# Moving softmax and gate exponentials from PSUM to SBUF in a two-block transformer kernel

## The reference

```
s = einsum('bqkgd,bskd->bkgqs', qblk, keys) * ATTN_SCALE
p = softmax(s, axis=-1)
o = einsum('bkgqs,bskd->bqkgd', p, vals)
```

```
la    = log_sigmoid(r @ w_d + b_d) / 16
bcum  = cumsum(la)                         # within a chunk
o     = (q * exp(bcum)) @ S  +  att @ v     # att: decayed q k^T, masked
S     = exp(b_last) * S + (k * exp(b_last - bcum))^T @ v
```

## Time and profile before

| | us |
|---|---|
| median of 3 runs | 4646.35 |
| lowest, highest | 4640.53, 4651.82 |
| the profiled execution, its own time | 4640.53 |
| its span, first to last instruction | 4638.7 |
| PE busy | 4180.4 (90%) |
| POOL busy | 1790.5 (39%) |
| DVE busy | 1612.5 (35%) |
| ACT busy | 1024.4 (22%) |
| mean granted clock of TensorE | 0.932 of full speed |

### The profile page before, as it was taken

How to read it: one execution, slowest core, us unless ns; L and a number is a source line. 1 busy time by engine, 2 the same in 40 slices (tenths; PEclk the granted TensorE clock), 3 DMA queues, 4 the chain that set the end, 5 groups by cost and what they waited for, 6 DMA issues and landing times. The chain is left out here.

```text
span 4638.7 us, 54497 instructions
## 1 busy us (share of the span) xinstructions
PE 4180.4 (90%) x20233; PEld 3195.3 (69%) x20233; DVE 1612.5 (35%) x2553; ACT 1024.4 (22%) x1739; POOL 1790.5 (39%) x770
## 2 busy tenths in 40 slices
PE   6899999999899987798999998886988988988999
PEld 5677788888789876566777776664854554866844
DVE  1333334655511141433255553343133334121100
ACT  1333122122200011333122221002144343001100
POOL 1333343233254452343544336664511110876700
PEclk7999999999999988899999998888888887999999
DMA  6111221111155532122322213233311100333332
GB/s 173 40 47 44 76 45 48 41 44 44 62 107 101 103 104 63 38 50 51 79 53 55 51 48 84 71 90 99 94 30 30 30 26 0 94 101 73 95 77 72
DMA packets 511988, 305.18 MB, mean 66 GB/s; under 512 B 37721, under 2 KB 492770, under 8 KB 511162
## 3 DMA queue, kind: packets, MB, share of 16 engines
q1 hardware_dynamic: 499706, 282.43, 24.9%
q10 hardware_dynamic: 12096, 20.33, 1.2%
HBM read 276.42 MB, written 26.27 MB: 65 GB/s over the span
## 5 line engine op out<-in xcount | busy, mean ns | idle before, releaser
L813 POOL TENSOR_TENSOR whi<-ring,con 128x1024 fp32r<-128x1024 f32 (+2 forms) x383 | 892.9, 2331 | 2572.1 <-DMA ring<-in_w_in 2087.0
L507 PE MATMUL ps<-xT_parts,whi 128*128 128x512 f32 (+2 forms) x2600 | 995.4, 383 | 124.0 <-DVEq L1945 71.7
L507 PE MATMUL ps<-hT_parts,whi 128*128 128x512 f32 (+1 forms) x2856 | 1047.8, 367 | 0.0
L507 PE MATMUL ps<-xT_parts,ring_parts 128*128 128x512 f32 (+2 forms) x2600 | 946.2, 364 | 0.0
L815 POOL TENSOR_TENSOR ring_parts<-ring,whi 128x1024 fp32r<-128x1024 f32 (+2 forms) x383 | 899.8, 2349 | 30.0
L1474 ACT ACTIVATE arena<-ps 128x512 f32<-128x512 f32 (+10 forms) x575 | 306.6, 539 | 2407.4 <-PE ps L507 1602.5
L507 PE MATMUL ps<-arena_parts,whi 128*128 128x512 f32 (+1 forms) x2112 | 630.8, 376 | 98.6 <-DVE arena_parts L1983 56.1
L507 PE MATMUL ps<-arena 128*128 128x128 f32 (+10 forms) x3324 | 675.9, 348 | 41.0 <-DVE arena L1951 36.4
L507 PEld LDWEIGHTS ps<-xT_parts,whi 128*128 128x128 f32 (+1 forms) x2600 | 495.9, 191 | 222.1 <-DVEq L1945 63.7
L507 PEld LDWEIGHTS ps<-hT_parts,whi 128*128 128x128 f32 x2856 | 543.5, 190 | 98.0 <-issue 8.4
L507 PEld LDWEIGHTS ps<-arena 128*128 128x128 f32 (+3 forms) x3324 | 450.7, 195 | 190.5 <-issue 138.5
(11 more groups left out here) (136 smaller groups left out, 3654.4 us busy)
## 6 DMA issues: line engine op xcount, KB each, us to landing
ring<-in_w_in SPq DMA_DIRECT2D x504, 256.0 KB, 3.9
arena<-in_w_ada SPq DMA_DIRECT2D x64, 256.0 KB, 4.9
ring<-in_w_up SPq DMA_DIRECT2D x64, 256.0 KB, 3.9
ring<-in_w_down SPq DMA_DIRECT2D x64, 256.0 KB, 3.9
ring<-in_w_out SPq DMA_DIRECT2D x48, 256.0 KB, 3.8
gates_kept<-stage ACTq DMA_DIRECT2D x24, 384.0 KB, 3.9
arena<-gates_kept SPq DMA_DIRECT2D x24, 384.0 KB, 3.6
ring<-in_w_ada SPq DMA_DIRECT2D x32, 256.0 KB, 3.9
```

Source lines behind the costliest of these rows:

```text
L507: return nc.tensor.matmul(o, l, r, start=first, stop=last)
L813: v.tensor_tensor(hi, raw, ones[:, 0:m].unsqueeze(1).to_broadcast([P, kt, m]), ALU.mult).then_inc(w_rounded, 1)
```

## The change

- The exponential of the attention scores is written to `prob` in SBUF; DVE's multiplication then works in place in `prob`. `scores(t)` waits for exp_done in place of prob_done, and the wait for a free `prob` slot goes from DVE to ACT.
- `gE` becomes an SBUF buffer. ACT's exponential reads the sums from PSUM and writes them there; `decayed` reads it there. `exponents` waits for e_ready in place of qk_ready, `levels` for e_ready as well, and ACT's `exponentials(j)` for qk_ready of the unit before.
- `decays` moves from after the second token tile to behind all of them; on ACT `copy_values(gv)` moves ahead of the decay chain.
- PE's wait for wd_in moves from `decays` to the start of the layer's GLA, ahead of `all_read()` and of the queries' tile.

```diff
+        gE = take(9, P)
...
-        gE = bank(2, 9 * P).rearrange("p (c m) -> p c m", c=9)
...
-                        pe.wait_ge(prob_done, u0 + t)
+                        pe.wait_ge(exp_done, u0 + t)
...
                 turned_tile(hP, ALL, m=32)
+                pe.wait_ge(wd_in, 64 * (l + 1))
                 all_read()
...
-                    def decays():
-
-                        pe.wait_ge(wd_in, 64 * (l + 1))
-                        pe.wait_ge(grs_ready, hh * 2)
-                        pe.wait_ge(s_ready, u0)
-                        for d in range(2):
-                            for t in range(NT):
-                                last = mm(bank(4 + 2 * d, 1024)[:, t * P:(t + 1) * P], gr[0:33, t * P:(t + 1) * P],
-                                          gwd[0:33, d, i * P:(i + 1) * P], True, True)
-                        last.then_inc(dec_done, 1)
-
-                    two_token_tiles(NT, {1: [decays]})
+                    two_token_tiles(NT)
+
+
+                    pe.wait_ge(grs_ready, hh * 2)
+                    pe.wait_ge(s_ready, u0)
+                    for d in range(2):
+                        for t in range(NT):
+                            last = mm(bank(4 + 2 * d, 1024)[:, t * P:(t + 1) * P], gr[0:33, t * P:(t + 1) * P],
+                                      gwd[0:33, d, i * P:(i + 1) * P], True, True)
+                    last.then_inc(dec_done, 1)
                     turned_tile(hP)
...
-                        pe.wait_ge(qk_ready, u0 + j)
+                        pe.wait_ge(e_ready, u0 + j)
                         pe.wait_ge(kN_ready, u0 + j)
...
                         pe.wait_ge(qk_ready, u0 + j + 1)
 
+                        pe.wait_ge(e_ready, u0 + j + 1)
...
-                        pe.wait_ge(qk_ready, u0 + NU)
+                        pe.wait_ge(e_ready, u0 + NU)
...
-                        do(bank(6, w), bank(6, w), ACT.Exp, scale=HD ** -0.5, bias=stat[:, t % 2, 1:2],
+
+                        if t >= 2:
+                            act.wait_ge(turned, u0 + t - 1)
+                        else:
+                            act.wait_ge(pv_done, hn)
+                        do(prob[:, t % 2, 0:w], bank(6, w), ACT.Exp, scale=HD ** -0.5, bias=stat[:, t % 2, 1:2],
...
+                    copy_values(gv)
                     act.wait_ge(dec_done, hh + 1)
...
-                    copy_values(gv)
                     p = product()
...
-                        e = gE if units[j][2] else gE[:, 0:9:8]
-                        do(e, e, ACT.Exp).then_inc(e_ready, 1)
+
+                        act.wait_ge(qk_ready, u0 + j)
+                        if units[j][2]:
+                            ins = do(gE, bank(2, 9 * P).rearrange("p (c m) -> p c m", c=9), ACT.Exp)
+                        else:
+                            ins = do(gE[:, 0:9:8], bank(2, 2048).rearrange("p (c m) -> p c m", c=2)[:, :, 0:P], ACT.Exp)
+                        ins.then_inc(e_ready, 1)
...
-                        if t >= 2:
-                            dve.wait_ge(turned, u0 + t - 1)
-                        else:
-                            dve.wait_ge(pv_done, hn)
-                        v.tensor_scalar(prob[:, t % 2, 0:w], bank(6, w), st[:, 3:4], None, ALU.mult).then_inc(prob_done, 1)
+                        pr = prob[:, t % 2, 0:w]
+                        v.tensor_scalar(pr, pr, st[:, 3:4], None, ALU.mult).then_inc(prob_done, 1)
```

## The result

The changed kernel takes 4788.78 us (median of 4 runs, 4777.92 to 4791.47), the kernel before 4644.12 in the same comparison: ratio 1.0305, interval 1.0284 to 1.0326, or 132 to 151 us more. The prediction was 4791 us. One execution in all the runs, of e8 and at a granted clock of 0.55, took 7064.84 us; no ratio in this document uses it. The profiled execution of the changed kernel was its fastest, 4768.78 us (span 4767.0), and the sum of the prediction was made against the profiled execution of before: 151 predicted, 128 found between the two.

What follows compares the result with a forecast made beforehand. PE (TensorE) was taken to bound the kernel, with almost no idle time to win. 102 + 26 + 17 + 11 - 5 = 151 us on the profiled 4640.5 us gave 4791 us; the range was 4700 to 4840.

Steps and rivals of the forecast that it cites:

- The wait edits, 0: Changed semaphore waits of PE and ACT: other waits in PE's order already cover them, so 0 us.
- gE, predicted 102 + 26 (the clock): Scan stages: DVE's gE multiplies wait for POOL's splits, 102 us (bounds 20 to 102), plus 26 us of lost clock.
- the meeting: A unit's gE multiply starting inside a POOL split instruction: 24 of 48 units in layer 0, 15 of 32 in layer 1.
- only the remainders count: Lower bound for gE: multiplies wait only for the POOL instruction in progress, its other half not getting between: 20 us.
- rival (1): Scan stages: meetings cost only the remainder, 20 us, without clock loss; +43 in all, 4683 us; chance 0.10.
- rival (4): Scan stages: the meetings move out of phase as all starts shift once; +3, no change, 4644 us; chance 0.03.
- The clock, 26 us: Scan stages: 15 PE stalls over 2.6 us each lose 1.7 us to a lower granted clock; bounds 0 and 65.
- Rival (2): Scan stages: all stalls cost clock, +40 more, 4831 us; chance 0.08.
- rival (3): Heads' starts: the decays' move pays in full, 17 us; -9 in all, 4631 us; chance 0.03.
- prob, 17: Attention: DVE's multiply on prob in SBUF waits for POOL; 14 tiles stall 20 us, 17 net; bounds -3 and +29.
- wd_in, 11: Start of each layer's GLA: PE waits 3.6 us for DMAs plus 1.7 of clock, 11 us; bounds 6 and 12.
- The decays, -5: Eight heads' starts: a 1.2 us gap goes, but the decay chain then delays exponents(0); -5 us, bounds 0 and -17.

Runs made afterwards that it cites:

- e8: Kernel before (gE in PSUM) with the two 128x1024 multiplies of a full unit merged into one DVE instruction: 4645.70 us, ratio 1.0004.
- e5: The whole change with each of POOL's two split instructions cut into halves: 4638.75 us, ratio 0.9999 to the kernel before.
- e7: Kernel before with gE in SBUF alone and the two multiplies of a full unit merged into one DVE instruction: 4667.15 us, ratio 1.0044.
- e1: Kernel before with gE in SBUF and its semaphore waits alone: 4767.32 us, ratio 1.0265.
- e2: Kernel before with prob written by ACT to SBUF alone, scores(t) waiting for exp_done: 4659.15 us, ratio 1.0036.
- e11: Kernel before with POOL's split instructions cut into halves and prob in SBUF: 4594.36 us, ratio 0.9905.
- e3: Kernel before with PE's wait for wd_in moved ahead of the queries' tile alone: 4653.89 us, ratio 1.0024.
- e4: Kernel before with the decay matmuls behind the token tiles and the gv copy ahead of the decay chain alone: 4640.95 us, ratio 0.9995.
- e6: Kernel before with POOL's split instructions cut into halves and nothing else: 4588.12 us, ratio 0.9884.
- e10: Kernel before with POOL's split instructions cut into halves and the decay matmuls moved behind the token tiles: 4586.65 us, ratio 0.9880.
- e12: The whole change without its gE edit (gE back in PSUM with the waits it had): 4669.73 us, ratio 1.0059 to the kernel before.

## Why the prediction held, point by point

**The wait edits, 0.** PE's rows of waits for ACT did not grow (80.3 and 4.2 us after, 90.9 and 4.9 before), and ACT's exponential of 1152 columns takes 1134 ns, 1115 before. Nothing contradicts 0; that they cost nothing by themselves was not tried alone.

**gE, predicted 102 + 26 (the clock).** The mechanism is right: the meeting, its lock to every second unit of layer 0 (23 + 14 units are hit, where I had 24 + 15; by my own count, L2194 starting inside a POOL instruction, it was 14 in layer 1 already before, and in a fifteenth the POOL instruction starts between the two multiplies), and the second multiply behind POOL's other half, which e5 and e7 show from two sides. My lower bound for it, "only the remainders count", was 20 us; e7, which is that case, measured 20. I took the upper bound, and the measured time lies below it. Of the alternatives, rival (1) and rival (4) fall with e1. The size of the waiting was too high: 79 us added in the change and 85 in e1, for 102. (e1's whole time, 123 with 111 to 136, does hold 128.) Two things make it up. A blocked multiply needs 1.07 to 1.09 us after POOL's end, not its full 1.21, and L815 needs 2.20 once its turn comes, not 2.36. The second multiply costs 2.15 more than unhindered (3.36 - 1.21), the first its remainder less 0.14: a hit costs about 0.35 us less than I priced, 13 us over 37. And PE's gaps are 1.8 us each in layer 0 (40.8 over 23 hits) where I had a mean stall of 2.2 over 24. In layer 0 this is such a unit; PE's gap after it is 2.54:

```profile
672.39 2.40 POOL L813 TENSOR_TENSOR whi<-ring,con 128x1024 fp32r<-128x1024 f32 x1 [11.18 <-DMA ring<-in_w_in]
672.48 3.39 DVE L2201 TENSOR_TENSOR arena<-arena 128x1024 f32<-128x1024 f32 x1
...
674.87 3.20 POOL L815 TENSOR_TENSOR ring_parts<-ring,whi 128x1024 fp32r<-128x1024 f32 x1
```

The Trainium skill, page "SBUF — State Buffer", section "Who interferes with whom", has the exclusion that the trace shows. What the trace adds is the order: the instruction queued next gets its turn between two instructions of the other engine, and here that is worth five times the rest. The 65 ns that the page "VectorE: DVE Perf Modes" of the same skill would save on an operand from SBUF do not appear: 1217 ns after, 1212 before. The same section of that page says itself that its 58 cycles are too few and that about 150 were measured; 1217 ns less a column a cycle is 150 ns, or 144 cycles.

**The clock, 26 us, from 15 stalls over 2.6 us at 1.7 each.** After, 11 gaps before L1185 are over 2.6 us. Behind 10 of them the granted clock falls, 18.7 us of work in all; behind the 33 of 0.3 to 2.6 us it falls once. In e1 it is 11 of 13, and 4 of 30. All five of those shorter gaps are over 2.0 us; behind the 49 gaps of 0.3 to 2.0 us in the two traces the clock never falls, and behind the 14 of 2.0 to 2.6 us five times. (In e5 it falls once behind a gap of 1.94 us, so 2.0 is no fixed edge.) PE after a gap of 4.02 us, the stage behind it, and the stage behind the 2.54 of layer 0, in the tables of windows:

```profile
2416.45 0.48 PE L1185 MATMUL ps<-con,arena 128*128 128x128 f32 x1 [4.02 <-DVE arena L2202]
2417.00:2423.00 6.00, 6.00 (x23) 4.49 (x23) 2.59 (x2) 0.23 (x1) 0.00 (x0) 0.59 0.00 0
679.50:685.50 6.00, 6.00 (x37) 4.74 (x36) 4.48 (x5) 1.41 (x2) 0.00 (x0) 1.00 0.00 1
```

The price of a gap holds on the mean, 1.9 us for 1.7 (most show 1.7, two of the ten nearly 2.9); the number of long stalls was too high, since the stalls were. Rival (2), that all of them cost clock, falls; rival (3), faster, falls with the result. The gap of 3.47 us at 2574.09 is the exception, with 1.00 behind it.

**prob, 17.** e2 gives 17. L2125 after, min/median/max ns:

```profile
L2125 DVE TENSOR_SCALAR arena<-arena,stat x80: 352/621/2791, 187.6 to 2278.1; 128x768 f32<-128x768 f32 x64, 128x256 f32<-128x256 f32 x16
```

The median is the 0.6 us that I took, the longest 2.8, within the "0.6 to 3" forecast. The mean of its 768-column form is 1003 ns beside 1018 before: busy time alone would call the edit free. That its wait is POOL's is supported by e11's waits, not shown by its time.

**wd_in, 11.** e3 gives 11. The gap in the first layer is 5.0 us instead of 0.95, against my 4.6:

```profile
609.99 0.79 PE L507 MATMUL ps<-xT_parts,whi 128*128 128x512 f32 x1 [4.96 <-DMA arena<-in_b_decay_bwd]
```

In the second layer it is 4.6. Behind both the clock falls, as I priced it: 0.76 and 0.72 over the next 6 us.

**The decays, -5.** This is the term that did not come out: it counted the idle time alone and took the matmuls behind the decays to keep their speed. The gap before the gk tile is gone, and the chain does hold `exponents(0)` by the predicted 0.5 us, but in one head of eight. In the other seven the granted clock falls right behind the decay matmuls, the gk tile (the keys' tile) takes about 1.5 us longer (3 us at 0.50 to 0.63), and the chain is done just before it. First head, then last, in the timeline of PE and in the tables of windows:

```profile
636.84 2.94 PE L507 MATMUL ps<-arena 33*128 33x128 f32 x24
639.78:642.78 3.00, 3.00 (x9) 2.40 (x9) 0.00 (x0) 2.91 (x3) 0.94 (x1) 0.57 1.18 221
650.86 1.52 PE L507 MATMUL ps<-con,arena 128*128 128x512 f32 x3 [0.95 <-DVE arena L1961]
...
2809.40:2812.40 3.00, 3.00 (x17) 2.53 (x16) 0.96 (x1) 2.97 (x4) 2.92 (x2) 1.00 0.06 10
2816.43 0.71 PE L507 MATMUL ps<-con,arena 128*128 128x128 f32 x4 [1.56 <-DVE arena L1961]
```

With clock 1.00 the last head shows 1.56 us before `exponents(0)`, 0.5 more than the 1.06 of the other heads of its layer. With 0.57 the first shows 0.95, as before the change. So in the whole change the move costs about 7 x 1.5 - 8 x 1.2 + 0.5 = 1 us instead of winning 5. Alone (e4) its time is not told from 0; in its profile the clock falls in 5 heads of 8. A fall at this place is not new with the change: before it, one head of the eight has it, the second of layer 1.

```profile
2424.30:2427.30 3.00, 3.00 (x17) 3.00 (x18) 1.22 (x2) 2.93 (x3) 0.06 (x1) 0.63 0.00 0
```

Why it comes so much more often after the move is open.

**The sum.** Against the profiled execution: 102 + 26 + 17 + 11 - 5 = 151 predicted, 128 found. The 23 us are, about, 23 of waiting for gE's multiplies (79 for 102) and 7 of clock behind them (19 for 26), less the 6 by which the decays missed in the other direction. Stage by stage it is the same: 16 in attention for 17, 109 in GLA for 134. Against the medians it is 145, because the profiled execution of the changed kernel was 20 us faster than its median.

## What to carry to other kernels

Before moving an operand from PSUM to SBUF, lay the DVE instruction's start times on the other engine's rows: what matters is whether both read SBUF at that moment, how long the other's instruction is, and whether two dependent DVE instructions leave a seam that it can slip into. Where they must share, cut the off-path engine's instructions in half (here 54 us off the kernel before; no other version of this study is faster by more than the noise) and merge those on the path (103 of e1's 123 us), and stop cutting when the starts make the other engine late itself. Price a stall by the clock too: gaps over 2.6 us before L1185 were followed by a clock loss of mostly 1.7 us in 21 of 24 cases in the profiles of the change and of e1, those of 2.0 to 2.6 us in 5 of 14, shorter ones in none. And look at the clock behind what you move, not at its idle time alone.

## What the runs showed of the hardware

- DVE instructions that read only SBUF and POOL's splits take turns, one instruction each, however long the one is: 2.20 us of POOL at 1024 columns, 1.13 at 512, and 2.14 of DVE's merged one in e7.
- The kernel before already paid for this: e6, which only cuts POOL's instructions, is 1.2% faster, though POOL was 39% busy and its splits seemed to have slack.
- The clock can fall without a gap: in the changed kernel it was 0.50 to 0.63 over the 3 us right behind the 33-row decay matmuls in 7 heads of 8, with PE busy 3.00 of 3.00 us. In the kernel before it is one head of 8 (0.63), in e4 and e10, which make the same move, 5 of 8, in e12 6 of 8. What decides it stays open.
